# Latent input product: two weight chunks together over each normalised tile, with the query's column sums and scale later in the third chunk

## The reference

```python
h = x @ w_in
c_q, c_kv, k_rope = jnp.split(h, [Q_LORA_RANK, Q_LORA_RANK + KV_LORA_RANK], axis=-1)
q = (rms_norm_2(c_q, g_q) @ w_uq).reshape(b, s, MLA_HEADS, QK_NOPE_DIM + QK_ROPE_DIM)
k_rope = apply_rope(k_rope, cos, sin)
kv = (rms_norm_2(c_kv, g_kv) @ w_ukv).reshape(b, s, MLA_HEADS, QK_NOPE_DIM + V_HEAD_DIM)
```

## Time and profile before

| | us |
|---|---|
| median of 3 runs | 2075.31 |
| lowest and highest run | 2071.68, 2075.44 |
| the profiled execution, its own time | 2070.44 |
| its span, first to last instruction | 2068.6 |
| PE busy in the span | 2000.0 (97%) |
| mean granted TensorE clock | 0.997 of full speed |

### The profile page before, as it was taken

The page is one execution under the profiler, slowest core; times in us unless marked ns, Lnnn a source line. Parts: engine busy times, 40 slices in busy tenths (PEclk is TensorE's granted clock), DMA queues, the critical chain, the costliest instruction groups (busy, mean ns, idle before and its releaser), DMA issues.

```text
span 2068.6 us, 23738 instructions
## 1 busy us (share of the span) xinstructions
PE 2000.0 (97%) x9691; PEld 1665.1 (80%) x9691; DVE 1266.7 (61%) x1566; ACT 860.2 (42%) x1253; POOL 987.7 (48%) x489
## 2 busy tenths in 40 slices
PE   6999999999999999999999999999998999999997
PEld 4777888788888877888888888878887888888886
DVE  8679737443254444662777775455589667777643
ACT  5747865621122236773433333242322243333322
POOL 5678754543443442114344444444667644444443
PEclk9999999999999999999999999999999999999999
DMA  6431131222222221111222332224222312232221
GB/s 206 175 122 69 62 120 64 82 82 102 102 82 102 102 79 44 39 55 61 82 85 99 102 102 84 99 95 160 82 74 100 142 63 90 94 102 102 85 99 41
DMA packets 35040, 193.00 MB, mean 93 GB/s; under 512 B 4399, under 2 KB 4991, under 8 KB 15412
## 3 DMA queue, kind: packets, MB, share of 16 engines
q1 hardware_dynamic: 34932, 191.49, 26.5%
HBM read 177.77 MB, written 13.64 MB: 93 GB/s over the span
## 4 chain that ended last, share of the span: by engine, by line
PE 81%; DVE 10%; POOL 4%; ACT 4%; issue 1%; DMA 0%; ACTq 0%; SPq 0%; DVEq 0%; POOLq 0%
PE ps L159 76%; PE ps L158 4%; DVE TMP L182 1%; DVE ps L194 1%; POOL WL L182 1%; DVE X L182 1%; PE ps L167 1%; DVE X L194 1%; DVE YL L182 1%; POOL CO L182 1%; POOL YF L182 1%; DVE VG L182 0%; DVE HL L194 0%; ACT PA L176 0%; POOL TMP L182 0%
## 5 line engine op out<-in xcount | busy, mean ns | idle before, releaser
L182 POOL TENSOR_TENSOR WL<-W,WH 128x2048 fp32r<-128x2048 f32 (+3 forms) x173 | 648.6, 3757 | 857.4 <-ACT WH L175 840.5
L159 PE MATMUL ps<-HH,WL 128*128 128x512 f32 (+1 forms) x1392 | 537.6, 386 | 11.8 <-DVE HL L194 5.0
L159 PE MATMUL ps<-HH,WH 128*128 128x512 f32 (+1 forms) x1392 | 531.7, 382 | 0.0
L159 PE MATMUL ps<-HL,WH 128*128 128x512 f32 (+1 forms) x1392 | 531.6, 382 | 0.0
L175 ACT ACTIVATE WH<-W 128x2048 fp32r<-128x2048 f32 (+2 forms) x145 | 267.7, 1846 | 316.0 <-PE ps L159 315.9
L159 PEld LDWEIGHTS ps<-HH,WL 128*128 128x128 f32 x1392 | 261.5, 188 | 68.9 <-POOL HL L182 8.3
L159 PEld LDWEIGHTS ps<-HH,WH 128*128 128x128 f32 x1392 | 261.5, 188 | 51.3
L159 PEld LDWEIGHTS ps<-HL,WH 128*128 128x128 f32 x1392 | 261.6, 188 | 49.7 <-issue 0.2
L182 DVE TENSOR_TENSOR MRL<-MID,MRH 128x512 fp32r<-128x512 f32 x76 | 177.4, 2366 | 162.4 <-ACT MRH L175 162.4
L159 PE MATMUL ps<-MRH,WL 128*128 128x512 f32 x608 | 238.2, 392 | 3.3 <-ACT PAD L175 2.2
L159 PE MATMUL ps<-MRH,WH 128*128 128x512 f32 x608 | 236.7, 389 | 0.0
(11 more groups left out here) (372 smaller groups left out, 3305.4 us busy)
## 6 DMA issues: line engine op xcount, KB each, us to landing
W<-in_up SPq DMA_DIRECT2D x44, 1024.0 KB, 4.8
W<-in_down SPq DMA_DIRECT2D x22, 1024.0 KB, 4.8
W<-in_w_up SPq DMA_DIRECT2D x16, 1024.0 KB, 4.8
W<-in_w_down SPq DMA_DIRECT2D x16, 1024.0 KB, 4.8
W<-in_hy_in SPq DMA_DIRECT2D x12, 1024.0 KB, 4.9
kd<-STG SPq DMA_DIRECT2D x36, 256.0 KB, 2.0
KB<-kd SPq DMA_DIRECT2D x8, 1024.0 KB, 6.1
W<-in_win_ag SPq DMA_DIRECT2D x4, 1024.0 KB, 5.1
```

Source lines behind the costliest of these rows:

```text
L159: return self.eng.matmul(out, lhs, rhs, start=start, stop=stop)
L182: return QUIET if self.eng is None else self.eng.tensor_tensor(out, a, b, op)
```

## The change

The product of the latent input takes chunks 0 and 1 as a pair; the column sums of `c_q` come after step 6 instead of step 3 of column tile 4, and the spread of their result after step 2 instead of step 0 of column tile 5.

```diff
             def within_in(n, k):
-                if (n, k) == (4, 3):
+                if (n, k) == (4, 6):
                     column_sum([(("cqs",), DG, ("cqadd", 1), None, None),
                                 (("cqs",), tmp("cq", 2), ("cqsq", 2), ("cq", 2), ("cqs",))])
-                if (n, k) == (5, 0):
+                if (n, k) == (5, 2):
                     spread("nq", slot=12)
 
-            gemm("mi", CH["mla_in"], 8, 2, feat, lambda k: ("hn", 3, k), within=within_in)
+            gemm("mi", CH["mla_in"], 8, 2, feat, lambda k: ("hn", 3, k), within=within_in, pair=True)
```

## The result

| | before | after |
|---|---|---|
| median of 14 runs, us | 2074.20 | 2077.97 |
| lowest and highest run, us | 2070.05, 2075.44 | 2074.61, 2079.96 |
| ratio, 95% interval | | 1.0020 [1.0012, 1.0028] |
| span of the profiled execution, us | 2068.6 | 2077.6 |
| its mean granted clock | 0.997 | 0.994 |

The change makes the kernel slower by 0.2%: the medians lie 3.8 us apart, and the interval reaches from 2.5 to 5.8 us. For the stretch that the change touches I compare inside one execution, from the first product of tile 0 to the first product of `uq`: 804.56 - 763.34 = 41.22 us before, 809.46 - 763.79 = 45.67 after, **+4.45 us**.

A forecast was written before the change was run, and what follows sets the result against it. PE, busy for 97% of the span, was taken as the bound. The terms -2.66 + 5.66 + 1.57 gave +4.6 us, so 2075.31 + 4.6 = 2079.9 us, with a range of 2074.7 to 2082.0.

The forecast's parts named there:

- The gain: Chunks 0 and 1 as a pair: PE waits for none of tiles 2 to 7 and ends 2.66 us earlier.
- The loss by the place: Chunk 2 reuses chunk 0's place, released 6.86 us later, so PE waits for its low half: 5.66 us lost.
- hand-over and restart: Small terms at chunk 2's start: 0.04 us from POOL's end to PE's start, 0.11 us of PE restart.
- The clock: After about 5.4 us idle ahead of chunk 2, PE runs at the lower clock level, losing 1.57 us.
- the early row: Earlier trace stretch: after 4.38 us idle, nine products took 3.72 us at granted clock 0.53; source of the 1.57 us.
- The sums: Column sums in chunk 2: the later place costs nothing; at the old place PE would wait 1.0 us.
- the clock would hold: Rival: full clock through the idle time ahead of chunk 2, total +3.0 us, 2078.3; chance 0.24.
- Four banks: Rival: the pair's cycling through four banks at each tile loses the clock, about +20 us, 2096; chance 0.01.
- later wait took the shift in: Rival: later waits absorb the shift, no net change; chance 0.03.

The follow-up runs named there:

- own_place_dve: The changed kernel with a place of its own for chunk 2 and its low half on DVE after the angle reduction; median 2070.45 us, ratio 0.9987.
- filler: The changed kernel with 20 products on spent data, results unused, between the pair and chunk 2; median 2076.57 us, ratio 1.0013.
- pair_sums_early: The changed kernel with the column sums and the spread back at their old places, only the pair left; median 2078.83 us, ratio 1.0024.
- low_dve_filler: The changed kernel with chunk 2's low half on DVE and 10 products on spent data ahead of chunk 2; median 2075.20 us, ratio 1.0011.
- low_dve: The changed kernel with chunk 2's low half made on DVE instead of POOL, its place still chunk 0's; median 2075.42 us, ratio 1.0013.

## Why the prediction was right

*The gain.* Predicted 2.66 us; own_place_dve, where nothing else is in the way, shows 2.66. The tiles came as forecast: one wait at tile 1, none behind it.

*The loss by the place.* Predicted 5.66 us with hand-over and restart. PE's gap is 791.74 - 785.97 - 0.23 = 5.54 us, and filler against own_place_dve (the same gain, no slow clock in either) gives 44.32 - 38.56 = 5.76, of which 0.11 is filler's later start of chunk 2. ACT began 7.33 us later by the trace's times, of which 0.45 came with tile 0, so 6.88 against a forecast of 6.86.

*The clock.* Predicted 1.57 us from the early row; filler shows 1.35 to 1.46. The slow stretch had seven products, not nine. It was the right kind of loss, a little oversized, and the term that makes 4.6 out of the measured 4.45 us.

*The sums.* The forecast said that at their old place PE would wait 1.0 us for them. That step failed: pair_sums_early shows no wait. The 1.0 us was worked out at full clock, while the sum itself had the first products of chunk 2 slow; the slow products delay PE by 1.35 to 1.46 us, more than the wait. In pair_sums_early POOL's sum ends at 795.65 (794.36 + 1.29), 0.38 us before PE gets there. The step had no weight in the sum, but low_dve_filler shows that the queue behind ACT's wait was the next thing late: with the clock held up and the low half early, 1.20 us came back there.

*The time.* The shift was 3.8 us by the medians and 4.45 by the trace, against 4.6. The rest of the distance from 2079.9 to 2077.97 is the base: 14 runs of the kernel before have a median 1.1 us below that of the three that the forecast started from. The forecast gave 0.55 to slower and 0.41 to the same, with 4.15 us as what a measurement can tell; 3.8 lies just below that, though the ratio's interval does not reach 1. A slip in the sum carries no weight: 2070.44 + 4.6 is 2075.0, not 2075.1.

*The rivals.* That the clock would hold is refuted for this idle time by the trace, and its price of +3.0 is what filler shows (+3.10). Four banks did not swing the clock, as the earlier trace rows had it: no product of the pair is slow. No later wait took the shift in: it is still +4.82, 0.45 of it from ahead of tile 0, at 1380.95.

## What to carry to other kernels

When work is regrouped so that two buffers are in use to the end of a group, look at who reuses the first of them: its release moves to the end as well, and the preparation behind it (here 1.9 us on ACT and 4.5 on POOL) loses its cover. The cost is the new delay less the old slack, and here one more buffer turned +0.20% into -0.11%, and with the low half on DVE as well into -0.13%. When a wait is shortened, count what stands behind it on the waiting engine too, since that queue is what is late next.

## What the runs showed of the hardware beyond that

The length of an idle time alone does not decide the clock. In low_dve 3.12 us ahead of chunk 2 lowered it. In the profiled execution of the changed kernel PE waited 3.63 us early on, and the stretch whose row before has 0.53 ran at 1.00 behind it. In that of filler PE waited 3.58 us at the same place, and the stretch ran at 0.50. The product of the timeline and the row of the stretch, for the changed kernel and then for filler (`issue`: the profile shows nothing that PE waited for):

```profile
25.14 0.47 PE L159 MATMUL ps<-HPH,WL 128*128 128x512 f32 x1 [3.63 <-issue]
```

```profile
25.10:28.70 3.60, 3.56 (x16) 2.93 (x16) 3.50 (x7) 0.72 (x3) 0.00 (x0) 1.00 0.01 3
```

```profile
25.22 0.77 PE L159 MATMUL ps<-HPH,WL 128*128 128x512 f32 x1 [3.58 <-issue]
```

```profile
25.10:28.70 3.60, 3.48 (x8) 2.84 (x9) 3.52 (x6) 0.72 (x3) 0.02 (x1) 0.50 0.01 3
```

And the waits of 2.44, 2.3 and 2.03 us behind 1380 left the clock alone before and lowered it after. So between 2.0 and 3.6 us of idle both outcomes stand in these traces, the same wait can go either way from one execution to the next, and the stretches behind such waits carry some 4 us of difference between single profiles of the same work. Differences of 0.1% need anchors within one execution, or many runs.
